# Front weights and transposed input laid out in one run per partition, small constant loads packed, first pieces halved: one decoder layer on one core

## The reference, cut to what matters

```python
proj = x @ w_in + b_in       # (256, 1024) @ (1024, 5192): q k v, indexer q k w, conv in, two gates
score = sum_h w_idx[h] * relu(q_idx[h] @ k_idx)          # indexer, 8 heads
sel = top_k(where(causal, score, -inf), 64)
bias = rel_bias[t5_bucket(q_pos - sel)]                  # (32, 8) table, by distance
logits = q @ k_sel * HEAD_DIM**-0.5 + bias
y_attn = softmax(logits) @ v_sel @ w_o_attn
y_conv = silu(layer_norm(depthwise31(a * sigmoid(g)))) @ w_o_conv
mix = (sigmoid(g_attn) * y_attn + sigmoid(g_conv) * y_conv) @ w_out
x = layer_norm(alpha * x + mix)
h = alpha * x + sum_e gate[e] * expert_e(x)              # w_gate_up 8 MB, w_down 4 MB for each of 32
x = layer_norm(h + sigmoid(h @ w_pg) * (p @ w_pp))
```

## Time and profile before

| | |
|---|---|
| median of three executions | 1175.26 us |
| profiled execution | span 1173.0 us; what lies around the span is in the metric, 2.3 us from the median |
| PE busy | 1134.9 us, 97% of the span |
| DVE / ACT / POOL busy | 299.7 / 173.6 / 11.4 us |
| moved by DMA | 448.16 MB, mean 382 GB/s; q1 439.79 MB, q10 7.38 MB |
| chain that ended last | PE 78%, DMA 18%, DVE 2%, ACT 1%, issue 1% |

### The profile page before, as it was taken

One profiled execution on the slowest core, in us unless ns is written; L12 is line 12 of the kernel. 1 busy time (PEld: TensorE's weight loads), 2 busy tenths in 40 slices (PEclk: granted clock), 3 DMA queues, 4 the chain that ended last, 5 costly groups with the idle time before them and its releaser, 6 DMA issues.

```text
span 1173.0 us, 13754 instructions
## 1 busy us (share of the span) xinstructions
PE 1134.9 (97%) x5620; PEld 573.9 (49%) x5620; DVE 299.7 (26%) x775; ACT 173.6 (15%) x336; POOL 11.4 (1%) x26
## 2 busy tenths in 40 slices
PE   9999999999999999999889999999999989999997
PEld 7888888734344343434234343443434333334346
DVE  0639842521113111111110211121111111111126
ACT  1213230211111111101010111111111010111112
POOL 0110000000000000000000000000000000000000
PEclk9999999999999999999999999999999999999999
DMA  9996367599999999999999999999999999999970
GB/s 319 353 325 233 109 276 297 217 405 377 430 430 430 431 428 431 429 430 430 429 426 428 430 423 433 429 432 426 434 430 430 430 429 429 423 428 427 425 329 37
DMA packets 60328, 448.16 MB, mean 382 GB/s; under 512 B 6656, under 2 KB 35616, under 8 KB 40544
## 3 DMA queue, kind: packets, MB, share of 16 engines
q1 hardware_dynamic: 52704, 439.79, 90.4%
q10 hardware_dynamic: 7552, 7.38, 1.9%
HBM read 444.53 MB, written 2.62 MB: 381 GB/s over the span
## 4 chain that ended last, share of the span: by engine, by line
PE 78%; DMA 18%; DVE 2%; ACT 1%; issue 1%; SPq 0%; ACTq 0%; DVEq 0%
PE bank L441 45%; DMA arena<-in_w_gu 17%; PE bank L711 10%; PE bank L460 5%; PE bank L418 4%; PE bank L858 2%; PE bank L871 2%; PE bank L1253 2%; PE bank L447 2%; ACT arena L1435 1%; PE bank L784 1%; DMA arena<-in_w_in 1%; PE bank L435 1%; PE bank L1126 1%; PE bank L1186 0%
## 5 line engine op out<-in xcount | busy, mean ns | idle before, releaser
L441 PE MATMUL bank<-arena 128*64 128x512 f32 x3168 | 695.3, 595 | 18.7 <-DMA arena<-in_w_gu 16.3
L441 PEld LDWEIGHTS bank<-arena 128*64 128x64 f32 x3168 | 233.8, 137 | 443.2 <-issue 407.0
L480 DVE TENSOR_TENSOR arena<-bank,arena 128x512 f32<-128x512 f32 x33 | 22.8, 692 | 685.7 <-PE bank L447 685.6
L711 PE MATMUL bank<-arena 128*128 128x256 f32 (+1 forms) x544 | 117.8, 377 | 0.5 <-DMA arena<-in_w_in 0.5
L711 PEld LDWEIGHTS bank<-arena 128*128 128x128 f32 x544 | 101.9, 190 | 15.0 <-DMA arena<-in_w_in 1.1
L1435 ACT ACTIVATE arena<-bank 128x512 f32<-128x512 f32 x62 | 37.0, 597 | 402.8 <-PE bank L441 402.8
L460 PE MATMUL bank<-arena 64*128 64x512 f32 x272 | 67.8, 616 | 0.7 <-ACT arena L1438 0.7
L418 PEld LDWEIGHTS bank<-sel,arena 128*128 128x128 f32 x480 | 54.7, 192 | 11.4 <-issue 11.4
L418 PE MATMUL bank<-sel,arena 128*128 128x128 f32 x480 | 57.6, 278 | 0.0
L1438 ACT ACTIVATE arena<-bank 128x512 f32<-128x512 f32 x32 | 19.1, 597 | 210.3 <-PE bank L441 210.3
L1636 DVE SCALAR_TENSOR_TENSOR arena<-arena 128x256 f32<-128x256 f32 x120 | 48.5, 479 | 0.5 <-DVE arena L1636 0.2
(11 more groups left out here) (213 smaller groups left out, 477.4 us busy)
## 6 DMA issues: line engine op xcount, KB each, us to landing
arena<-in_w_gu SPq DMA_DIRECT2D x45, 4096.0 KB, 31.2
arena<-in_w_dn SPq DMA_DIRECT2D x60, 2048.0 KB, 33.3
arena<-in_w_gu SPq DMA_DIRECT2D x33, 2048.0 KB, 38.7
arena<-in_w_in SPq DMA_DIRECT2D x19, 1024.0 KB, 12.8
arena<-in_w_gu SPq DMA_DIRECT2D x9, 1024.0 KB, 9.1
arena<-in_w_dn SPq DMA_DIRECT2D x6, 1024.0 KB, 9.9
arena<-in_w_out SPq DMA_DIRECT2D x4, 1024.0 KB, 5.1
arena<-in_w_pg SPq DMA_DIRECT2D x2, 2048.0 KB, 32.4
```

Of the source, the lines that this page charges most:

```text
L441: mm = pe.matmul(to[half * CAP:(half + 1) * CAP, :], rows, w[:, half * 512:(half + 1) * 512], start=first, stop=last)
L711: mm = pe.matmul(bank[n % 4][:, lo:S], w[:, k, j * P:(j + 1) * P], xT_sb[:, k, lo:S], start=(k == 0), stop=(k == KD - 1))
```

## The change

Host side, the weights of the front are stored chunk by chunk. Within a chunk all that a partition needs lies together: 8 runs of 1 KB become one run of 8 KB (chunks of `w_oa` and `w_oc`: 4 runs of 2 KB become one of 8 KB; chunk 2: 8 runs of 288 bytes become one of 2304 bytes). Chunk 1 alone is stored in four quarters, 4 runs of 2 KB for each partition. xT and chunk 0 come in five parts of 1, 1, 2, 2 and 2 depth blocks, one run for each partition in each part. pT becomes one run of 2 KB for each partition.

`bT`, `bki`, `bwi` and `passes` become one load, `consts1`; `dwT`, `convT`, `b_r`, `ln1T`, `bguT` and `w_r` become one, `consts2` (3808 bytes for each partition); `relb` and `onehot` become one. PE does four warm-up products, not five, and the table product stands behind chunk 1, no longer ahead of it. Addresses of small buffers move. The table write, its two skewed loads, x, and all of the experts are as before.

```diff
+FIRST_PARTS = ((0, 1), (1, 1), (2, 2), (4, 2), (6, 2))
...
@@ SP
-                what, c0, n = FRONT[0]
-                for quarter in range(4):
-                    sp.dma_start(w_view(0)[:, 2 * quarter:2 * quarter + 2, :],
-                                 src[what][2 * quarter * P:(2 * quarter + 2) * P, c0:c0 + n].rearrange("(k p) c -> p k c", p=P)
-                                 ).then_inc(first_in[quarter], 16)
+                n = FRONT[0][2]
+                for part, (k0, kn) in enumerate(FIRST_PARTS):
+                    sp.dma_start(wslot(0)[:, k0 * n:(k0 + kn) * n],
+                                 w_in[P * k0 * n:P * (k0 + kn) * n].rearrange("(p m) -> p m", p=P)
+                                 ).then_inc(first_in[part], 16)
...
-                    sp.dma_start(w_view(i), src[what][:, c0:c0 + n].rearrange("(k p) c -> p k c", p=P)
-                                 ).then_inc(arrived[i % NS], 16)
+                    flat, at, size = chunk_at(i)
+                    runs = flat[at:at + P * size]
+                    if i == 1:
+                        sp.dma_start(wslot(i)[:, 0:size].rearrange("p (q m) -> p q m", q=4),
+                                     runs.rearrange("(q p m) -> p q m", q=4, p=P)).then_inc(arrived[i % NS], 16)
+                    else:
+                        sp.dma_start(wslot(i)[:, 0:size], runs.rearrange("(p m) -> p m", p=P)
+                                     ).then_inc(arrived[i % NS], 16)
...
@@ PE
-                for _ in range(5):
+                for _ in range(4):
                     pe.matmul(bank[7][:, 0:S], warm[:, 0:P], warm, start=True, stop=True)
...
-                pe.wait_ge(relb_in, 32)
+                two(1, TOPK)
+                pe.wait_ge(relb_in, 16)
                 pe.wait_ge(relb_copied, 1)
                 pe.matmul(bank[7][:, 0:S + P], relb_copies, oneh_sb[:, :], start=True, stop=True).then_inc(tab_done, 1)
-                two(1, TOPK)
...
@@ ACT
-                a.dma_start(relb_sb[:, :], relb).then_inc(relb_in, 16)
-                a.dma_start(oneh_sb[:, :], onehot).then_inc(relb_in, 16)
-                a.dma_start(bT_sb, bT).then_inc(small_in, 16)
-                a.dma_start(bki_sb, bki).then_inc(small_in, 16)
-                a.dma_start(bwi, b_in[WI0:WI0 + 8].partition_broadcast(P)).then_inc(small_in, 16)
-                a.dma_start(pass_c, passes).then_inc(small_in, 16)
-                a.wait_ge(first_in[3], 16)
+                a.dma_start(early_consts, consts1).then_inc(small_in, 16)
+                a.dma_start(relb_and_onehot, relb).then_inc(relb_in, 16)
+                a.wait_ge(first_in[4], 16)
+                a.dma_start(late_consts, consts2).then_inc(late_in, 16)
                 a.dma_start(vb, b_in[V0:V0 + 512].partition_broadcast(P)).then_inc(late_in, 16)
...
-                a.dma_start(bgu, bguT.rearrange("p (e f) -> p e f", e=NE)).then_inc(late_in, 16)
                 a.dma_start(x_sb, x.rearrange("(t p) d -> p t d", p=P)).then_inc(x_in, 16)
-                a.dma_start(pT_sb, pT.rearrange("(k p) t -> p k t", p=P)).then_inc(ple_in, 16)
+                a.dma_start(pT_sb, pT.rearrange("p (k t) -> p k t", k=2)).then_inc(ple_in, 16)
```

More of the change, by code:

```diff
@@ L78, in up, with program @@
         return self.n
-def program(nc, x, xT, pT, w_in, bT, bki, b_in, w_oa, w_oc, w_out, dwT, convT, ln1T, ln1g, ln1b, w_r, b_r,
-            w_gu, bguT, w_dn, b_dn, w_pg, w_pp, ln2g, ln2b, relb, onehot, passes, out, table):
+def program(nc, x, xT, pT, w_in, consts1, consts2, b_in, w_oa, w_oc, w_out, ln1g, ln1b,
+            w_gu, w_dn, b_dn, w_pg, w_pp, ln2g, ln2b, relb, out, table):
     F32, I32 = mybir.dt.float32, mybir.dt.int32
@@ L192, in program @@
[L192 to L205, removed]
+        o += NE
+        early_consts = view(o, 47)
+        bT_sb, bki_sb, bwi = view(o, 36), view(o + 36, 1), view(o + 37, 8)
+        pass_c = view(o + 45, 2)[0:MORE, :]
+        above, expert_no = pass_c[:, 0:1], pass_c[:, 1:2]
+        bq = view(o + 47, 4)
@@ new lines, in program @@
+        o += 51
+        late_consts = view(o, 952)
+        dw = view(o, 124).rearrange("p (a j) -> p a j", a=4)
+        cv = view(o + 124, 12).rearrange("p (j a) -> p j a", j=3)
+        br = view(o + 136, NE)
+        ln1_col = view(o + 168, 2 * KD)
+        bgu = view(o + 184, NE * 16).rearrange("p (e f) -> p e f", e=NE)
+        wr_sb = view(o + 696, KD * NE).rearrange("p (k e) -> p k e", k=KD)
+        o += 952
+        wsc = view(o, 16).rearrange("p (t h) -> p t h", t=NT)
+        top8 = view(o + 16, 16).rearrange("p (t h) -> p t h", t=NT)
@@ new lines, in program @@
+        mv = view(o + 32, 4).rearrange("p (t h) -> p t h", t=NT)
+        rstd = view(o + 36, 2)
+        mx = view(o + 38, 16).rearrange("p (t h) -> p t h", t=NT)
+        ssum = view(o + 54, 16).rearrange("p (t h) -> p t h", t=NT)
+        epsc = view(o + 70, 1)
+        o += 71
+        NEP = NE + 2
+        mask = view(o, NT * NEP).rearrange("p (t e) -> p t e", t=NT)
+        gate = view(o + 68, NT * NEP).rearrange("p (t e) -> p t e", t=NT)
+        slot1 = view(o + 136, NT * NEP).rearrange("p (t e) -> p t e", t=NT)
@@ L225, in program @@
         small_in, late_in = sem("small_in"), sem("late_in")
-        xT_in, x_in = [sem(f"xT_in{i}") for i in range(4)], sem("x_in")
-        first_in = [sem(f"first_in{i}") for i in range(4)]
+        xT_in, x_in = [sem(f"xT_in{i}") for i in range(len(FIRST_PARTS))], sem("x_in")
+        first_in = [sem(f"first_in{i}") for i in range(len(FIRST_PARTS))]
         warm_ready, no_index = sem("warm_ready"), sem("no_index")
@@ L296, in program, with chunk_at @@
         src = {"in": w_in, "oa": w_oa, "oc": w_oc, "out": w_out}
+        def chunk_at(i):
+            what, _, n = FRONT[i]
+            depth = 4 if what in ("oa", "oc") else KD
+            return src[what], P * depth * sum(m for w, _, m in FRONT[:i] if w == what), depth * n
         def wait_chunk(eng, i):
@@ L582, in into_ring @@
                     early(n, piece)
-                for i, (what, c0, n) in enumerate(FRONT):
-                    if i == 0:
-                        continue
+                for i in range(1, NF):
                     if i == 25:
@@ L717, in _ @@
                 pe.wait_ge(warm_ready, 1)
-                for _ in range(5):
+                for _ in range(4):
                     pe.matmul(bank[7][:, 0:S], warm[:, 0:P], warm, start=True, stop=True)
                 for k in range(KD):
-                    if k % 2 == 0:
-                        pe.wait_ge(xT_in[k // 2], 16)
-                        pe.wait_ge(first_in[k // 2], 16)
+                    for part, (k0, _) in enumerate(FIRST_PARTS):
+                        if k == k0:
+                            pe.wait_ge(xT_in[part], 16)
+                            pe.wait_ge(first_in[part], 16)
                     for j in range(2):
@@ L1588, in _ @@
                                         ).then_inc(chosen, 1)
-                v.wait_ge(late_in, 16 * 7)
+                v.wait_ge(late_in, 32)
                 v.wait_ge(tab_ready, 1)
@@ L1954, in turned_rows, with by_depth, chunk_major, copied @@
         return a.reshape(2, P, 4, -1).transpose(0, 2, 1, 3).reshape(a.shape)
+    def by_depth(a, parts):
+        a = _np.asarray(a)
+        a = a.reshape(-1, P, a.shape[1])
+        return _np.concatenate([a[k0:k0 + kn].transpose(1, 0, 2).reshape(-1) for k0, kn in parts])
+    def chunk_major(what, a):
+        whole, quarters = ((0, a.shape[0] // P),), [(k0, 2) for k0 in range(0, KD, 2)]
+        return _np.concatenate([by_depth(a[:, c0:c0 + n], FIRST_PARTS if i == 0 else quarters if i == 1 else whole)
+                                for i, (w, c0, n) in enumerate(FRONT) if w == what])
+    def copied(a):
+        return _np.broadcast_to(_np.asarray(a)[None, :], (P, len(a)))
+    def side_by_side(*pieces):
+        return _np.concatenate([_np.asarray(a, dtype=_np.float32) for a in pieces], axis=1)
     b = _np.asarray(b_in[0])
@@ L1958 @@
     given = {
-        "x": by_rows(x[0]), "xT": _np.asarray(x[0]).T, "pT": _np.asarray(p[0, 0]).T, "w_in": w_in[0],
-        "bT": _np.concatenate([rows(a) for a in placed], axis=1),
-        "bki": _np.concatenate([b[KI0:WI0], b[KI0:WI0]])[:, None], "b_in": b,
-        "w_oa": w_o_attn[0], "w_oc": w_o_conv[0], "w_out": by_rows(w_out[0]),
-        "dwT": _np.asarray(w_dw[0]).T.reshape(4, P, CW).transpose(1, 0, 2).reshape(P, 4 * CW),
-        "convT": _np.concatenate([rows(a[0]) for a in (b_dw, conv_ln_g, conv_ln_b)], axis=1),
@@ L1965 @@
-        "ln1T": _np.concatenate([rows(turned_rows(a[0])) for a in (ln1_g, ln1_b)], axis=1),
-        "ln1g": by_rows(ln1_g)[0], "ln1b": by_rows(ln1_b)[0], "w_r": turned_rows(w_router[0]), "b_r": b_router[0],
-        "w_gu": w_gate_up[0], "bguT": _np.asarray(b_gate_up[0]).reshape(NE, 2, 2, P, 4).transpose(3, 0, 1, 4, 2).reshape(P, NE * 16), "w_dn": w_down[0],
+        "x": by_rows(x[0]), "xT": by_depth(_np.asarray(x[0]).T, FIRST_PARTS),
```

(10 more changed lines are left out.)

64 lines of the change are left out of this document (28 added, 36 removed).

## The result

The changed kernel took 1190.03 us (median of 4 runs, 1189.28 to 1191.67), the kernel before 1175.35 us in the runs beside them; ratio 1.0127, 95% interval 1.0115 to 1.0139. It is slower, 14.7 us where 10.2 were forecast, and the time lies 0.03 us over the end of the stated range, 1190. The span of the profiled execution is 1187.5 us, 1173.0 before.

What follows compares the result with a forecast made beforehand. PE work bounds the kernel from 13.01 us, behind chunk 1's load. A late table write costs 8.8 us of PE waiting plus 1.4 for the clock, 10.2 together: 1185.5 us, own range 1181 to 1190, stated range 1174.5 to 1190.

Steps and rivals of the forecast that it cites:

- The alternation packet by packet: Backlogged queues q1 and q10 take turns one packet each, whatever the sizes; 1408 q10 packets go beside 8 KB ones.
- the table write as victim: On q10, the table write, 1024 packets of 1.5 KB, was to land at 51 us instead of 34.3.
- ACT's order as what passes it on: ACT waits for `tab_out` before indexer head 4; two DMA issues, relus and an evacuation PE needs stand behind that wait.
- tile 10 as PE's stop: PE was to begin tile 10, the first of chunk 6, at 55.0 us instead of 46.2: 8.8 us lost.
- the clock behind it: After an idle stretch of 9 us PE restarts at a granted clock of 0.50, costing 1.4 us.
- the transfer of the front's loss to the end: A microsecond won or lost in the front is one at the end; expert weights shift with PE.
- Rival A: Packets don't alternate one for one, or q1 runs dry; table lands near 29 us, total 1174.8 us; chance 0.18.
- Rival B: The start wins much more, at most 2.9 us, with no table stall: 1172.4 us; chance 0.04.
- rival C: The skewed loads also come late, landing at 98 us and costing about 15 us more: 1200 us; chance 0.04.
- Where does x begin?: When the load of x starts moving on q10, behind `consts2` and `vb`: 14 us, bounds 12 to 16.
- The next term: Transfer of x, pT and the table on q10 beside 8 KB packets: 14.4 MB at 412 GB/s, 35.0 us.
- The start: PE's first chunks: chunk 1 lands at 11.6 us, chunk 2 begins at 18.0 instead of 18.48, gaining 0.5 us.

Runs made afterwards that it cites:

- e1_front_2k: The changed kernel with chunks 3 to 20 of the front weights in four runs of 2 KB, not one of 8 KB: 1176.62 us, ratio 1.0013.
- e3_skew_late: The changed kernel with ACT's wait for `tab_out` and the two skewed loads moved behind the evacuation of kT: 1176.74 us, ratio 1.0013.
- e2_before_8k: The kernel before with only chunks 2 to 28 of the front weights in 8 KB runs, small loads left unpacked: 1194.5 us, ratio 1.0164.
- h2_after_quarters: The changed kernel with chunk 0 and xT in four parts and five warm-up products: 1188.79 us, ratio 1.0115.
- f2_quarters: e1_front_2k with the table product back ahead of chunk 1, chunk 0 and xT in four parts, five warm-up products: 1174.37 us, ratio 0.999.
- e4_x_behind: The changed kernel with the loads of x and pT issued directly behind the table write: 1187.24 us, ratio 1.0101.
- h1_x_last: The changed kernel with the loads of x and pT issued behind the evacuation of kT, so behind the skewed loads: 1182.74 us, ratio 1.0061.

## Why the prediction was wrong in size

**Direction, place and mechanism held.** The alternation packet by packet, the table write as victim, ACT's order as what passes it on, tile 10 as PE's stop, the clock behind it, and the transfer of the front's loss to the end all stand in the trace, and e1_front_2k and e3_skew_late each took the loss away by one of the links. Rival A (bytes shared, or no backlog) failed at its condition: 193 packets against 194. The Trainium skill's advice to coalesce (DMA: Bandwidth & Descriptors, Rules for kernel authors), named beside it, isn't refuted by that. It speaks of small transfers, and e2_before_8k, which leaves them apart, was slower still. What it doesn't tell is the price of longer runs on the neighbour queue. The other rule of that page, turns by packets in Queues, rings and completion order, is borne out at 2, 4, 8 and 16 KB on q1. But the page has a typical packet hold some 9 to 17 descriptors (orders for one piece each), and in these rows a turn is one contiguous run, of whatever size. Rival B did not occur: chunk 2 began later, not sooner. Nor did rival C: the skewed loads landed 8.6 and 10.9 us behind their issue, and POOL didn't wait for them.

**The step that failed** is "Where does x begin? ... I take 14 us (12 to 16)". The first 4 KB packets of x went at about 20.8 us. The loads on q10 of the changed kernel were: `vb` issued at 10.44 and landed 10.8 us later, at 21.2; x issued at 12.02, landed after 17.7, at 29.7. Three parts of that term were mis-sized. The last part of chunk 0 landed at 10.05, not near 9. Then q10 stood still: `consts2` was issued at 10.06 and its first packet moved 3.7 us later, at about 13.75, though q10 sent nothing else from 12 us on; I had no term for that. From 14 us on the queues alternate. The rows are q1 and q10 from 12 to 14, then from 14 to 16 us:

```profile
q1 hardware_dynamic: 182, 0.80, 100.1%
q10 hardware_dynamic: 12, 0.05, 5.7%
```

```profile
q1 hardware_dynamic: 80, 0.57, 68.6%
q10 hardware_dynamic: 76, 0.29, 35.9%
```

And I had costed the 128 packets of 3.8 KB of `consts2` at nothing, though they alternate with q1's like all the others: 128 x (8192 + 3808) bytes at 420 GB/s are 3.7 us. The very load that the change makes by packing is part of what delays the table. With the 3.2 us for `vb`: 10.05 + 3.7 + 3.7 + 3.2 = 20.65.

**The next term was too long instead:** 35.0 us for x, pT and the table; from 20.8 to 52.5 (2.0 us ahead of the landing, as in the prediction) it took 31.7. q1 was backlogged all that time, but its packets were on average shorter than 8 KB. From 21 to 52 us it moved 1400 packets with 10.18 MB, 7.3 KB each, beside 1397 of q10. In the row from 36 to 40 us 21 of q1's 193 packets are under 512 bytes, and the other 172 account for its 1.41 MB. They fit 16 small ones for each chunk of 128 runs, so presumably each DMA ends with them; that isn't shown. They take a turn too, so q10 gets more turns than there are weight packets. `tab_out` came at 54.47 instead of 51: the start of x was taken 6.8 us too early and the transfer 3.3 us too long, which leaves 3.5. The second error hid half of the first, which is luck.

**The rest:** from `tab_out` to tile 10 4.16 us (3.97 forecast), and the clock 1.7 (1.4). Tile 10 began at 58.63 where it began at 46.2 before: 12.4 us later, where I had 8.8. PE idled for 11.25 of these 12.4; the rest is mostly the late start, which would have been a loss without the wait too. 12.4 + 1.7 = 14.1, plus 0.4 in the experts, 14.5 in the span. The bounds took 16 us as the latest start of x and so ended at 1190.4; the stated range cut that to 1190. The four runs spread from 1189.28 to 1191.67, so nothing hangs on the 0.03 us: what was wrong is that the bounds of x's start, 12 to 16, left out 20.8.

**The start** went to the other side of its value: 0.5 us gain forecast, and chunk 2 began 0.9 us late in the changed kernel (18.58 + 0.85 against 18.48). I had taken the rate of before as a floor for larger runs; the halved first pieces broke it (307 GB/s from 5 to 7 us, 369 before). And the moved table product lay on the path, while PE's idle time for chunk 1 (1.14 us in the changed kernel) would have held it. That the start doesn't count while PE waits for the table was right (h2_after_quarters). In all parts of the change but three (8 KB runs in chunks 3 to 20, five parts with four warm-ups, table product behind chunk 1) there is a gain: f2_quarters is the fastest kernel of the study, 0.1% under the kernel before, with an interval that just leaves out no change.

## What to carry to other kernels

Before the packets of one DMA queue are made larger, count the packets of the other. While both are backlogged they take turns one for one, as they did here at every size, so a transfer of 1024 short runs on the other queue takes 1024 turns of the new length, and everything ahead of it on its queue takes its turns first. Count all that stands ahead, the new packed loads too, and the time from an issue to its first packet. A wait for such a transfer belongs behind the work that others need from the same engine; moved there, the same late transfer cost nothing. And a DMA issue isn't always cheap: look at how long it held its engine when much is queued.

## What the runs showed of the hardware that I had not expected

- From an issue on ACT to its first packet 3.5 to 3.7 us went by, though what stood ahead on q10 was through within 2 us: `consts2` in the changed kernel, the table write in e4_x_behind and h1_x_last. Why isn't shown.
- An issue on ACT mostly took 0.35 to 0.6 us, but 2.23 to 7.09 us for five of the issues behind `w_r` in e2_before_8k, 4.73 for pT behind the table write and x in e4_x_behind, and 4.81 for its second skewed load. What sets it is open, and it isn't the count of packets alone: in the kernel before, x was issued behind `w_r` in 0.46 us at 13.43, 6 us before `w_r` landed.
- With longer runs SP's issues are cheap: a chunk of `w_in` took a median of 3.18 us (up to 8.23) to issue in 1 KB runs, and 0.46 (up to 1.57) in 8 KB runs.
- Two parts of 128 KB and three of 256 KB on each queue moved 257 to 312 GB/s from 5 to 7 us in seven kernels, four parts of 256 KB 404 and 407.
- After 3.86, 8.01, 11.08 and 11.25 us of idle time the clock cost PE's next 32 instructions 2.8, 2.5, 3.0 and 1.7 us (h1_x_last, e4_x_behind, h2_after_quarters, the changed kernel); the kernel before had 1.4 behind 4.28 us. The cost doesn't follow the length of the pause. In h2_after_quarters the granted clock was still 0.50 from 62 to 63 us, 5 us after PE had resumed; in the changed kernel it was 1.00 there, 4 us after.
